# Gate and up of a feed-forward block by Strassen's seven products, the way back in three parts

## The reference, cut to what matters

```python
    x = x + merged @ w_out                                  # "out2", 1024 x 1024
    h = rms_norm(x, ffn_norm)
    gate, up = jnp.split(h @ w_ffn_in, 2, axis=-1)          # 1024 x 5632: 2816 gate, 2816 up columns
    return x + (jax.nn.silu(gate) * up) @ w_ffn_out         # 2816 x 1024
```

## Time and profile before

| | |
|---|---|
| median of three runs | 2333.64 us |
| the profiled execution | 2336.28 us, span 2334.6 us |
| mean granted clock of TensorE | 0.98 of full speed |
| TensorE matmuls busy | 2221.2 us, 95% |
| weight loads | 1683.0 us, 72% |
| Vector / Scalar / GpSimd busy | 1240.0 / 844.0 / 354.4 us |
| HBM traffic | 123 GB/s over the span |

### The profile page before, as it was taken

The page is one execution under the profiler, slowest core; times in us unless marked ns, Lnnn a source line. Parts: engine busy times, 40 slices in busy tenths (PEclk is TensorE's granted clock), DMA queues, the critical chain, the costliest instruction groups (busy, mean ns, idle before and its releaser), DMA issues.

```text
span 2334.6 us, 28101 instructions
## 1 busy us (share of the span) xinstructions
PE 2221.2 (95%) x10765; PEld 1683.0 (72%) x10765; DVE 1240.0 (53%) x2363; ACT 844.0 (36%) x1486; POOL 354.4 (15%) x273
## 2 busy tenths in 40 slices
PE   7999999779898999999999999999999999999999
PEld 4885677643335776777888888887677787888887
DVE  4743445651226777665654434459766755443442
ACT  4444442421112446434332222344554433332221
POOL 0111023000001455331000000025443200000000
PEclk9999898879999999999999999999999999999999
DMA  8216310289996232221323323232222123323322
GB/s 302 60 55 216 118 37 10 105 334 410 409 409 234 74 90 55 73 76 42 99 91 100 99 90 105 82 99 73 73 62 75 56 72 100 100 90 100 100 81 81
DMA packets 175580, 288.01 MB, mean 123 GB/s; under 512 B 13486, under 2 KB 125656, under 8 KB 175448
## 3 DMA queue, kind: packets, MB, share of 16 engines
q1 hardware_dynamic: 173152, 278.73, 35.5%
q0 software_dynamic: 1152, 4.19, 0.5%
q10 hardware_dynamic: 1144, 3.29, 0.4%
HBM read 281.98 MB, written 4.19 MB: 123 GB/s over the span
## 4 chain that ended last, share of the span: by engine, by line
PE 79%; DVE 10%; DMA 5%; ACT 3%; issue 2%; SPq 1%; POOL 0%; DVEq 0%; ACTq 0%
PE PS L677 21%; PE PS L679 20%; PE PS L678 20%; PE PS L1451 3%; PE PS L2440 3%; PE PS L2479 2%; PE PS L1433 2%; PE PS L2499 1%; PE PS L1443 1%; PE PS L1618 1%; PE PS L1628 1%; DMA AR<-in_w_mod_dram 1%; SPq L3634 1%; PE PS L1100 1%; DMA ONCE<-in_w_gate_dram 1%
## 5 line engine op out<-in xcount | busy, mean ns | idle before, releaser
L677 PE MATMUL PS<-OPH,WHI 128*128 128x512 f32 x1224 | 499.1, 408 | 13.9 <-DVE AR L1288 5.0
L679 PE MATMUL PS<-OPH,WLO 128*128 128x512 f32 x1224 | 481.9, 394 | 0.0
L678 PE MATMUL PS<-OPL,WHI 128*128 128x512 f32 x1224 | 480.9, 393 | 0.0
L628 ACT ACTIVATE WHI<-RAW 128x1024 fp32r<-128x1024 f32 (+2 forms) x282 | 292.8, 1041 | 457.3 <-PE PS L679 449.1
L649 DVE TENSOR_TENSOR WLO<-RAW,WHI 128x1024 fp32r<-128x1024 f32 (+1 forms) x187 | 224.2, 1201 | 373.8 <-ACT WHI L628 373.7
L665 POOL TENSOR_TENSOR WLO<-RAW,WHI 128x1024 fp32r<-128x1024 f32 (+1 forms) x95 | 229.5, 2418 | 952.9 <-ACT WHI L628 946.9
L677 PEld LDWEIGHTS PS<-OPH,WHI 128*128 128x128 f32 x1224 | 232.1, 190 | 81.2 <-issue 28.0
L679 PEld LDWEIGHTS PS<-OPH,WLO 128*128 128x128 f32 x1224 | 232.0, 190 | 50.4
L678 PEld LDWEIGHTS PS<-OPL,WHI 128*128 128x128 f32 x1224 | 232.6, 190 | 43.5 <-issue 1.0
L677 PE MATMUL PS<-WHI,OPH 128*128 128x512 f32 (+2 forms) x568 | 228.4, 402 | 7.9 <-DVE OPL L2140 2.4
L679 PE MATMUL PS<-WHI,OPL 128*128 128x512 f32 (+2 forms) x568 | 216.0, 380 | 0.0
(11 more groups left out here) (446 smaller groups left out, 3255.1 us busy)
## 6 DMA issues: line engine op xcount, KB each, us to landing
RAW<-in_w_in_dram SPq DMA_DIRECT2D x102, 512.0 KB, 3.7
RAW<-in_w_ffn_in_dram SPq DMA_DIRECT2D x88, 512.0 KB, 3.5
RAW<-in_w_ffn_out_dram SPq DMA_DIRECT2D x40, 512.0 KB, 3.4
RAW<-in_w_mod_dram SPq DMA_DIRECT2D x36, 512.0 KB, 4.6
ONCE<-in_w_down_dram SPq DMA_DIRECT2D x35, 512.0 KB, 15.8
RX<-in_w_gate_dram SPq DMA_DIRECT2D x33, 512.0 KB, 15.6
RAW<-in_w_out_dram SPq DMA_DIRECT2D x24, 512.0 KB, 3.5
ONCE<-in_w_up_dram SPq DMA_DIRECT2D x20, 512.0 KB, 14.9
```

The costliest lines, as they stand in the source:

```text
L628: hi.up(A.e.activation(q.fhi, q.flat, ACT.Copy), ("w", q.i))
L677: T.e.matmul(o, a[0], b[0], start=first, stop=False)
L678: T.e.matmul(o, a[0], b[1], start=False, stop=False)
L679: return T.e.matmul(o, a[1], b[0], start=False, stop=last)
```

## The change

One group of columns (the first) stays as it was. The other ten are each computed as a 2x2 block product: W11 and W21 are the upper k-half (blocks 0 to 3) of the gate and of the up columns, W12 and W22 the lower k-half (4 to 7), and the tokens are cut in two halves T1 and T2 of 256. Four sums of weights and four sums of activations turn the eight block products into seven, with 256 columns moving and an output of two 128x256 halves in one PSUM bank (Winograd's form of Strassen's scheme).

- The four raw pieces of a group are loaded in the order W11, W21, W22, W12; they aren't split as they are. Vector makes four sums of 128x1024 (`s1` to `s4`: two into `SUMS[0]` and `SUMS[1]`, one in place over W21, one over `SUMS[1]`). Seven "steps" are split in place of four pieces: Scalar the high parts, GpSimd the low parts of steps 0, 1, 3 and 4, Vector those of 2, 5 and 6. Half places stay three, raw places become five (`FIFTH`); `ahead` replaces `i + 3` and counts only pieces and steps that are split.
- The activation sums `TR` are made once per layer, beside the `out2` stage (8 Scalar and 16 Vector operations of 128x256), then split: four high parts on Scalar, two low parts each on Vector and GpSimd, at the beginning of the feed-forward stage.
- Out of PSUM: Scalar copies product 0 (`E1`), Vector adds products 1, 2, 3, 4, 5, 6 and once more 2 (`c22`) into `E2`, `G2` and `U2`. The root is then applied in SBUF: to gate by Vector (128x1024), to up by GpSimd (two halves of 128x512). Silu, product, high and low part are now one operation of 128x1024 each, and are issued during the next group's products 0 to 2.
- The way back runs after groups 3, 7 and 10 (8, 8 and 6 hidden blocks; before 12 and 10), with the same number of matmuls and eight more additions to `XT` a layer. The first two weight sums of the next group are issued before the last column pair of the way back.

The core of the diff:

```diff
-        for f, (c0, c1) in enumerate(((0, 12), (12, 22))):
-            J["ffi", l, f] = [(plan(d["w_ffn_in_2"][l][:, 128 * m:128 * m + 256], 4, 256, True), ...
+        for c in range(11):
+            wg, wu = (d["w_ffn_in_2"][l][:, n0 + 256 * c:n0 + 256 * c + 256] for n0 in (0, 2816))
+            if c == 0:
+                J["ffi", l] = [ffn_pieces(wg, True, True), ffn_pieces(wu, True, True)]
+            else:
+                w11, w21, w22, w12 = (seq[ffn_pieces(x, False)[0]] for x in (wg[0:512, :], wu[0:512, :], wu[512:1024, :], wg[512:1024, :]))
+                J["step", l, c] = st = [ffn_step(w11.flat, w11, None, True), ffn_step(SUMS[1], w11, ("s2", l, c), True),
+                                        ffn_step(SUMS[0], w11, ("s1", l, c), False), ffn_step(w21.flat, w21, ("s3", l, c), True),
+                                        ffn_step(w12.flat, w12, None, True), ffn_step(w22.flat, w22, None, False),
+                                        ffn_step(SUMS[1], w12, ("s4", l, c), False)]
+            if c in (3, 7, 10):
+                w = d["w_ffn_out_2"][l][1024 * (c // 4):256 * c + 256, :]
...
+        def pe_unit(l, c):
+            products = ((own(0, T1), None, (glu_a, ("e1", l, c))), (summed_(1), 1, (glu_v, ("u2", l, c))),
+                        (summed_(0), 0, (glu_v, ("c22", l, c))), (summed_(2), 2, (glu_v, ("u3", l, c))),
+                        (own(4, T1), None, (glu_v, ("g1", l, c))), (summed_(3), 3, (glu_v, ("ut1", l, c))),
+                        (own(4, T2), None, (glu_v, ("gt2", l, c))))
+            for n, (moving, q, emptied) in enumerate(products):
+                s = take(J["step", l, c][n].i)
...
+                for j in range(2):
+                    for k in range(4):
+                        mm = mm3(ps(b)[:, 256 * j:256 * j + 256],
+                                 (s.hi[:, k, 128 * j:128 * j + 128], s.lo[:, k, 128 * j:128 * j + 128]),
+                                 moving(k), k == 0, k == 3)
...
+        def act_unit(l, c):
+            for n in range(7):
+                if n == 1:
+                    A.wait_ge(*prod["fp", l, c, 0])
...
+                    glu_a.up(A.e.activation(E1, half_banks(PB["fp", l, c, 0]), ACT.Copy), ("e1", l, c))
+                    if follows(c):
+                        act_silu(l, c - 1)
+                if n == 2 and follows(c):
+                    act_hidden(l, c - 1)
+                act_hi(ahead(J["step", l, c][n].i))
...
+        def dve_unit(l, c):
+            more = c + 1 < 11 and follows(c + 1)
+            for n in range(7):
+                if n == 0 and follows(c):
+                    dve_last_of(l, c - 1)        # evict product 6 of c-1, then G2 = G2 * RST (128x1024)
+                if n == 1:
+                    if follows(c):
+                        dve_act(l, c - 1)        # SLU2 = SLU2 * U2
+                    dve_fourth_sum(l, c)
+                if n == 2:
...
+                    glu_v.up(V.e.tensor_tensor(E2, bank(1), E1, ALU.add), ("u2", l, c))
+                    if follows(c):
+                        dve_act_low(l, c - 1)
+                if n == 3:                       # u4: bank(2) + E2 -> G2[T2]
...
+                if n == 4:                       # u3: bank(3) + E2 -> U2[T1]; c22: bank(2) + U2[T1] -> U2[T2]
...
+                if n == 5:
+                    glu_v.up(V.e.tensor_tensor(G2[:, :, T1], bank(4), E1, ALU.add), ("g1", l, c))
+                    if more:
+                        dve_two_sums(l, c + 1)
+                if n == 6:
+                    glu_v.up(V.e.tensor_tensor(U2[:, :, T1], bank(5), U2[:, :, T1], ALU.add), ("ut1", l, c))
+                    if more:
+                        dve_third_sum(l, c + 1)
+                dve_lo(ahead(J["step", l, c][n].i))
...
+        def pool_ffn(l):
...
+            for c in range(1, 11):
+                steps_ = J["step", l, c]
+                if c == 1 or not follows(c):
+                    pool_lo(steps_[0].i + 1)
+                    pool_lo(steps_[1].i + 1)
+                pool_lo(steps_[3].i + 1)
+                pool_lo(steps_[4].i + 1)
+                G.wait_ge(*glu_v["c22", l, c])
+                glu_p.up(G.e.tensor_tensor(U2[:, :, T2], U2[:, :, T2], root_of(T2), ALU.mult), ("u2", l, c))
+                if c + 1 < 11 and follows(c + 1):
+                    pool_lo(J["step", l, c + 1][0].i + 1)
+                    pool_lo(J["step", l, c + 1][1].i + 1)
+                G.wait_ge(*glu_v["ut1", l, c])
+                glu_p.up(G.e.tensor_tensor(U2[:, :, T1], U2[:, :, T1], root_of(T1), ALU.mult), ("u1", l, c))
```

More of the change, by code:

```diff
@@ L232, in body @@
         after, gain, twos = None, None, False
+        load, made, step, sums, since = True, None, None, None, None
     seq = []
@@ new lines, in body, with ffn_pieces, ffn_step @@
+        turn5 = [0]
+        def ffn_pieces(w, split, pool=False):
+            made_ = []
+            for k0 in range(0, w.shape[0], 512):
+                s = ring5[turn5[0] % 5]
+                turn5[0] += 1
+                made_ += plan(w[k0:min(k0 + 512, w.shape[0]), :], 4, 256, split, pool=pool,
+                              at=FIFTH if s == fifth else None, place=s)
+                if s == fifth:
+                    seq[made_[-1]].since = ("out2", l), 0
+            return made_
+        def ffn_step(flat, source, made_, pool):
+            q = Piece()
+            q.i, q.kc, q.n, q.split, q.pad, q.pool, q.load = len(seq), 4, 256, True, None, pool, False
+            q.flat, q.made, q.slot, q.loaded = flat, made_, source.slot, source.loaded
+            q.raw = flat.rearrange("p (k n) -> p k n", k=4)
+            h = nhalf[0] % NHL
+            nhalf[0] += 1
+            q.half_before = half_of[h]
+            half_of[h] = q
+            q.fhi, q.flo = WHI[:, 1024 * h:1024 * h + 1024], WLO[:, 1024 * h:1024 * h + 1024]
+            q.hi = q.fhi.rearrange("p (k n) -> p k n", k=4)
+            q.lo = q.flo.rearrange("p (k n) -> p k n", k=4)
+            seq.append(q)
+            return q
@@ L392, in body @@
+        nslot[0] = next(s for s in [ring5[(turn5[0] + x) % 5] for x in range(5)] if s != fifth)
     signals = []
@@ L3442, in pe_ffn @@
         def pe_ffn(l):
             for f, (c0, c1) in enumerate(PARTS):
[L3444 to L3468, removed]
@@ L3470, in hidden @@
-                def hidden(k):
-                    T.wait_ge(*glu_a["hi", l, c0 + k])
-                    T.wait_ge(*glu_v["lo", l, c0 + k])
-                pe_add_cols(("ffo", l, f), J["ffo", l, f], lambda k: pair(AF, (c0 + k) % 20), hidden, SQ5, f == 1 and l == 0)
+                for c in range(c0, c1):
+                    if c:
+                        pe_unit(l, c)
+                    else:
+                        pe_unit_plain(l)
+                def hidden(k):
+                    T.wait_ge(*glu_a["hi", l, c0 + k // 2])
+                    T.wait_ge(*glu_v["lo", l, c0 + k // 2])
@@ new lines, in pe_ffn, with act_silu, act_hidden @@
+                pe_add_cols(("ffo", l, f), J["ffo", l, f], lambda k: pair(AF, k), hidden, SQ5, f == 2 and l == 0)
+        def act_silu(l, c):
+            A.wait_ge(*glu_v["g", l, c])
+            if c:
+                A.wait_ge(*glu_v["lo", l, c - 1])
+            glu_a.up(A.e.activation(SLU2, G2, ACT.Silu), ("silu", l, c))
+        def act_hidden(l, c):
+            A.wait_ge(*glu_v["act", l, c])
+            if c >= 4:
+                A.wait_ge(*prod[("ffo", l, c // 4 - 1), 7])
+            glu_a.up(A.e.activation(AF[0][:, 2 * c % 8:2 * c % 8 + 2], SLU2, ACT.Copy), ("hi", l, c))
@@ L3492, in act_ffn @@
-                act_add_cols(("ffo", l, f), J["ffo", l, f], SQ5, f == 1 and l == 0, ("an", 1) if f == 1 and l == 0 else None)
+                for c in range(c0, c1):
+                    if c:
+                        act_unit(l, c)
+                    else:
+                        for pieces in J["ffi", l]:
+                            for i in pieces:
+                                act_hi(ahead(i))
+                act_silu(l, c1 - 1)
+                act_hidden(l, c1 - 1)
+                act_add_cols(("ffo", l, f), J["ffo", l, f], SQ5, f == 2 and l == 0, ("an", 1) if f == 2 and l == 0 else None, ahead)
@@ L3520, in dve_ffn @@
-                dve_add_cols(("ffo", l, f), J["ffo", l, f], None, *((("an", 1), SQ5) if f == 1 and l == 0 else ()))
+                for c in range(c0, c1):
+                    if c:
+                        dve_unit(l, c)
+                        continue
+                    dve_two_sums(l, 1)
+                    for j in range(2):
+                        V.wait_ge(*prod["fi", l, j, 0])
+                        glu_v.up(V.e.tensor_tensor(G2[:, j], ps(PB["fi", l, j, 0]), RST[:, :], ALU.mult),
+                                 ("gate", l, j), *([("g", l, 0)] if j else []))
+                    dve_third_sum(l, 1)
+                    for pieces in J["ffi", l]:
+                        for i in pieces:
+                            dve_lo(ahead(i))
```

(10 more changed lines are left out.)

255 lines of the change are left out of this document (200 added, 55 removed).

## The result

The changed kernel takes 2385.98 us (median of 4 runs, 2381.46 to 2389.01) where the kernel before took 2332.81 beside it (2323.94 to 2334.61): ratio 1.0234, 95% interval 1.0203 to 1.0265, so 53 us slower. Forecast were 2363 and a range of 2314 to 2400. The profiled execution took 2381.46 us, span 2380.0.

A forecast was written before the change was run, and what follows sets the result against it. TensorE's matmuls bound the feed-forward stage before; afterwards Vector and GpSimd taking turns would. Groups +11.4, ends +1.7 and token sums +1.7 make +14.8 us a layer, +29.6 in all: 2363 us, range 2314 to 2400.

The forecast's parts named there:

- TensorE bounds the stage: Feed-forward stage lasts as long as its matmuls; a group's seven products take 20.02 us for 21.76, at most 34.8 us gained.
- Rival E: Groups' products: narrow matmuls are slower between others, costing 34 us for each 10 ns; chance 0.03.
- The shared ports: Full groups: Vector operations with two SBUF inputs and GpSimd's take turns, needing 22.5 us against TensorE's 20.02.
- forecast C: Groups: Vector and GpSimd take turns, full groups 24.7 us; 2363 us in all, own range 2348 to 2394; chance 0.60.
- Rival A: Groups: GpSimd and Vector seldom meet, TensorE sets the pace, -28 us, 2306 us; chance 0.12.
- The walk: Groups, turn by turn: 24.7 us a full group (bounds 23.9 and 26.7), three parts together +11.4 us a layer.
- rival D: Groups: TensorE's waits of 2.2 us halve its clock, +10 to +35 us on top, say 2385 us; chance 0.13.
- Ends of the parts: Way back after each part: stalls of 0.1, 0.1 and 1.5 us before the last blocks, bounds 0 and 4 a layer.
- Token sums: Start of the feed-forward stage: token high and low parts delay a weight piece by 1.7 us, bounds 0 and 4.
- Rival B: Groups: perfect packing, the shared resource never idles, full groups 21.9 us; -13 us, 2321 us; chance 0.12.

The follow-up runs named there:

- the run with PSUM inputs: Changed kernel with Vector's ten 128x1024 operations a group taking their second input from PSUM, so not the block's result: 2302.43 us, ratio 0.9883.
- the two runs with late scaling: Changed kernel, all low parts on Vector, up's root scaling moved to the way back's output: 2307.62 us; the same with step 6's low part on GpSimd: 2305.06 us.
- The split alone: Kernel before with the way back in three parts (8, 8 and 6 hidden blocks), nothing else changed: 2332.17 against 2329.86 us, ratio 1.0011.
- the last one: Changed kernel with up scaled late and all low parts on Vector except step 6's, which is on GpSimd: 2305.06 us, ratio 0.9893.

## Why the prediction was right, point by point

- **TensorE bounds the stage and the narrow matmul costs 0.119 us.** Right: 0.120; 20.16 us for 20.02. Rival E is out. Twenty groups in which nothing is late gain 32 us. Of these 27 are left in the time of the run with PSUM inputs, 24 and 27 in the two runs with late scaling.
- **The shared ports** (forecast C). Right, and shown from both sides: take away Vector's second SBUF input, or GpSimd's work, and the loss is gone. The Trainium skill, SBUF — State Buffer (terms), has the pair of ports as an exclusive lock that an instruction holds to its end. The runs agree on the blocking, 3.43 us for 1.21. They also show that a second input in PSUM frees Vector of it, 1.21 to 1.22 beside a running low part. Rival A, that the two seldom meet, is out.
- **The walk: +11.4 us a layer for the groups.** This is the term that was mis-sized: measured +24.0 (75.2, 95.0 and 71.5 us for 65.3, 87.0 and 65.3) and, in the second layer, +24.9. The walk had product 4 about 0.5 us late; it was 2.65 late in 13 of the 14 groups from the second of a part on (not counting the group right behind the plain one). I had let GpSimd's turn for step 3 fall either before or after Vector's multiplication and took its being first as the better case (24.3 us a group), counting only the time in the ports. But the multiplication heads a chain over Scalar and back to GpSimd's next low part. With it first, and nothing else changed, the three parts of the first layer took 71.8, 92.4 and 68.1 us, near the 70.1, 91.8 and 67.1 of the walk, and the kernel gave back 28 of the 53 us.
- **Where the walk lost it.** Counted as it counts, from product 1 to product 1, the full groups of the first layer took 24.9 to 25.7 us for 24.7: they get part of the loss back, since product 1 of the next group is then only 0.6 to 1.5 us late and not 2.2. The last group of each part has no such wait to save, and took 20.5 to 22.0 for 18.9.
- **The clock** (rival D). It came true on top of C and not in its place: after 2.49 us of rest the next product lasted 4.2 to 4.4 us in place of 2.88 in 10 of the 13 places, about 1.4 us each, 14 us in all, and one more place had it ahead of product 1. I had given D a chance of 0.13 and asked for a gap near 3 us; shorter ones did.
- **Ends of the parts**: 1.7 us a layer forecast; the ways back took 44.0, 44.0 and 36.0 us, in which the third waits 1.5 at the hidden block's low part. Beyond their matmuls that is 4.4 us, where the two of before had 1.7; so 2.6 more, about 1 us over the forecast and inside its bounds. The split alone is within the noise.
- **Token sums**: 1.7 us a layer forecast, measured about 0.5 (plain group 23.1 us against 22.6). Why it was less no run here shows.
- **Rival B** (nothing idles, -13 us) would have needed each of GpSimd's operations at a spot where the ports lie idle. No run has that; the last one does it for the one low part that fits where Vector reads PSUM, and keeps no other on GpSimd.

So the mechanism and the sign were right and the size was about half: +29.6 forecast, +53 measured. That 2386 still lies inside C's own range (2348 to 2394) is in part luck. Its upper end stood for ports held for whole durations and for both stalls at their bounds of 4 us. Neither was seen: the multiplication of group 6 ended 1.08 us after GpSimd's low part, less than its own 1.21, and the stalls were 2.6 and 0.5. The late turn and the clock filled the room.

## What to carry to other kernels

Two engines that each have time to spare need not have it together. When work is given to GpSimd, add its time to that of Vector's operations with both inputs in SBUF, compare the sum with the time there is, and look for the stretch where Vector reads PSUM. Where queues in order and a shared port are both in play, ask of each turn what chain stands behind the loser, and not only how long the holder holds. A scaling that commutes with a product can leave the crowded stage for one with room: with all low parts on Vector, that took 2326.9 us to 2307.6, where the scheme had gained nothing with the scaling in its old place.

## What the runs showed of the hardware

- Operations of Vector and GpSimd of 1024 elements with both inputs in SBUF take turns, and the recorded duration of the one that loses includes its wait (Vector 1.21 to 3.43 us, GpSimd 2.39 to 3.38). A long Vector duration is thus a wait that no idle column shows.
- Vector's 128x1024 operation takes 1.21 to 1.22 us with the second input in PSUM and as long with it in SBUF where GpSimd stands still: the PSUM input cost nothing here.
- TensorE's granted clock fell to 0.50 (1.2 GHz in place of 2.4) after a rest of 2.49 us in 10 of 13 such places, as from 1372.00 to 1375.00. After the rests of up to 1.3 us ahead of product 1 in twelve of these groups it stayed at 1.00. After a rest of 1.93 us ahead of product 1 of group 2 it did either: 0.50 from 2034.00 to 2037.20 in the second layer, 1.00 from 1218.70 to 1222.00 in the first; and with two low parts on GpSimd half clock followed four of eight such rests. So a rest of a given length costs the clock in some places and not in others. Before the change the argument had one such case, a rest of 2.91 us.
